# Two-block transformer kernel: the first block's attention, with the values as the stationary side and the weights transposed by a diagonal

## The chip, the cores and the metric

One NeuronCore of a Trainium2 chip runs the whole program. Its engines are TensorE (PE in the rows; PEld is its weight load), VectorE (DVE), ScalarE (ACT), GpSimd (POOL) and SyncE (SP), which issues most DMAs. The metric is the device time of one execution in microseconds, as the median of several runs.

## The reference

A model of two blocks of two layers each, on one sequence of 256 tokens with width 1024, all in float32. The change touches the dilated attention in the layers of the first block (8 heads of 64). For one query position, the three dilated patterns together amount to one softmax in which a key counts once for each pattern that reaches it; the kernel puts the logarithm of that count into an additive mask. What is computed there:

```python
s = jnp.einsum('bnqhd,bnkhd->bnhqk', qb, kb) * (Dh ** -0.5)
s = jnp.where(mask[None, :, None], s, -jnp.inf)
m = jnp.max(s, axis=-1, keepdims=True)
p = jnp.exp(s - m)
l = jnp.sum(p, axis=-1)
o = jnp.einsum('bnhqk,bnkhd->bnqhd', p, vb) / jnp.transpose(l, (0, 1, 3, 2))[..., None]
...
wts = jax.nn.softmax(jnp.stack(lses), axis=0)
return jnp.einsum('gbsh,gbshd->bshd', wts, jnp.stack(outs))
...
mixed = ga * (ya @ w_proj_att) + gb * (yb @ w_proj_mlstm)
x = x + mixed @ w_out
```

`ya` is the attention's output, `yb` that of a second branch (an mLSTM) that runs beside it.

## The kernel before

The weights of all layers come through three slots as chunks of 128 x 2048 float32. SyncE loads a chunk into `raw`, ScalarE copies it to the reduced format fp32r as `w_hi` (L158), VectorE subtracts to get `w_lo` (L165), and PE multiplies with three products (L189 to L191) that keep float32 accuracy. A feature chunk (`f_chunk`, called through `feature(i, c)`) is 48 such products, and its result is the projection of the activations with features in the partitions. The order of work on each engine is written out by hand: between two feature chunks PE does one small step of the attention or of the mLSTM, so that the other engines have the length of a chunk to answer. `Splitter.upto(c)` on ScalarE (`high`) and VectorE (`low`) splits chunks up to number c. Semaphores carry the dependencies; a `Signal` counts them over the layers.

The attention in one layer l goes like this. The 256 queries are two tiles `qt`; tile 0 sees one tile of keys, tile 1 sees two.

- VectorE evicts the values from PSUM into `v_tok`, with a column of ones behind each head's 64 values (L812).
- PE writes the scores (L1114). VectorE adds the mask (L894) and takes the row maxima (L899, L901). ScalarE takes the exponentials in place in `logit` (`soft(qt)`, L634), a head at a time.
- PE transposes the weights in 24 tiles of 128 x 128, in three groups of eight (`weights_T(0)` to `(2)`, L1159): groups 0 and 1 are tile 1 of the queries, group 2 is tile 0. ScalarE copies each group to `pT` (L683).
- PE multiplies the transposed weights, as the stationary side, with values and ones (L1184): 24 products of 65 columns. The result has tokens in the partitions, and column 64 of each head is the row sum.
- VectorE takes the reciprocals of the sums (L970), multiplies into `ya` (L975), and PE transposes `ya` in eight tiles (L1191) to put the features into the partitions. ScalarE and VectorE split that into `yH` and `yL` (L697, L984), which the projection chunks 23 to 26 read.

The gate chunks between these steps are numbers 17 to 22: `feature(8, 17)`, `weights_T(0)`, `feature(9, 18)`, `weights_T(1)` and the transposes of `hn` (L1170), `feature(10, 19)`, `weights_T(2)`, `feature(11, 20)`, the value products, `feature(12, 21)`, the transposes of `ya`, `feature(13, 22)`. Meanwhile VectorE normalises the mLSTM's output: it waits for ScalarE's copies of the numerators (L667, L668), squares (L935), and goes through a chain of small instructions to `hn` (L953), for which `weights_T(1)` waits on PE. GpSimd only issues four kinds of DMA in the first block.

Of the kernel before, what the change touches and what calls it, by code (L numbers as in the profile page):

```python
# [48 lines left out]

DVE_A = 112  # L50


CARRIED = {n: n for n in ("sc_done", "pT_done", "pT_ready", "pv_done", "max_ready", "exp_ready", "mix_ready", "mixH_ready",
                          "mix_split", "f_evicted")}
CARRIED.update(xT_done="qkT_done", uv_done="yaT_done", hT_done="hnT_done", rbc_done="nm_done", up0_done="s_done",
               xH_ready="qkF_ready", x_ready="ya_split", nH_ready="yaH_ready", n_ready="yb_split")
# [346 lines left out]
def head_slot(h):  # L403


    return h // 2, h % 2
# [3 lines left out]
def first_block(nc, k, d, sems, block):  # L410

    with ExitStack() as ctx:
# [3 lines left out]
        def sig(name, per, start=0):  # L416
# [26 lines left out]
                R3[:, MH * SEQ:MH * (SEQ + P)].rearrange("p (h n) -> p h n", h=MH)]  # L443
        v_tok = sb("v_tok", [P, TT, AH, AD + 1])
        mv_tok = sb("mv_tok", [P, TT, MH, MD + 1])
# [3 lines left out]
        hn = sb("hn", [P, TT * MH * MD])  # L449
        ya = sb("ya", [P, TT * AH * AD])  # L450
        hn_v = hn[:, :].rearrange("p (t h d) -> p (t h) d", t=TT, h=MH)
# [3 lines left out]
        num_out = lambda tt, h: three(tt)[:, h, :] if h < 3 else fourth[:, tt, :]  # L455
        ya_v = ya[:, :].rearrange("p (t j e d) -> p t j e d", t=TT, j=4, e=2)
        g_rows = hn[0:MH, :].rearrange("p (a n) -> p a n", a=4)
# [11 lines left out]
        nL = k.mixL[:, :].rearrange("p (f n) -> p f n", f=8)  # L469
        yH, yL = k.aH, k.aL  # L470
        junk = R2[:, 0:TT * DM].rearrange("p (t n) -> p t n", t=TT)
        s2 = sb("s2", [P, TT])
# [29 lines left out]
            sig("hn_ready", 1), sig("hnT_done", 1), sig("yb_ready", 1), sig("ybH_ready", 1), sig("yb_split", 1))  # L502
        pT_done, pT_ready, pv_done, ya_ready = sig("pT_done", 3), sig("pT_ready", 3), sig("pv_done", 1), sig("ya_ready", 1)
        yaT_done, yaH_ready, ya_split = sig("yaT_done", 1), sig("yaH_ready", 1), sig("ya_split", 1)
# [16 lines left out]
        def _(pool):  # L521
# [3 lines left out]
                .then_inc(row_loaded.sem, 16)  # L525
            pool.dma_start(consts[:, KA_ADD:KA_END], d.consts_a[:, KA_ADD:KA_END]).then_inc(const_loaded.sem, 16)
            for l in range(1, DEPTH):
                pool.wait_ge(t_evicted.sem, t_evicted.at(l - 1, 4))
                pool.wait_ge(gate_ready.sem, gate_ready.at(l - 1, 1))
                pool.dma_start(rows[:, :], d.rows_a[l:l + 1, :].rearrange("a n -> (a n)").partition_broadcast(P))\  # L530
                    .then_inc(row_loaded.sem, 16)
                pool.wait_ge(k.a_ready.sem, k.a_ready.at(l - 1, 12))
                pool.dma_start(par[:, :], d.par_a[l * P:(l + 1) * P, :]).then_inc(par_loaded.sem, 16)
                if l == 1:
                    pool.dma_start(hot, d.hot_b).then_inc(hot_loaded.sem, 16)
                    pool.dma_start(rel_sb, d.rel_bias).then_inc(hot_loaded.sem, 16)
                    pool.wait_ge(line_ready.sem, 1)
                    pool.dma_start(d.bias_line, line).then_inc(k.bias_moved, 16)
# [3 lines left out]

            pool.dma_start(k.par_b, d.par_b[0:P, :]).then_inc(k.par_b_loaded, 16)
            pool.wait_ge(k.a_ready.sem, k.a_ready.at(DEPTH - 1, 12))
            pool.dma_start(consts[:, KB_ADD:KB_END], d.consts_b[:, KB_ADD:KB_END]).then_inc(k.consts_b_loaded, 16)
# [20 lines left out]
        def _(act):  # L566
# [6 lines left out]
            for l in range(DEPTH):  # L573
# [40 lines left out]
                def conv_tanh(j):  # L614
                    act.wait_ge(conv_ready.sem, conv_ready.at(l, j + 1))
                    act.activation((hn, ya)[j][:, :], mqk[:, 4 * j:4 * j + 4, :].rearrange("p f n -> p (f n)"),
                                   ACT.Tanh, scale=0.5).then_inc(convt_ready.sem, 1)
# [12 lines left out]
                def soft(qt):  # L630

                    act.wait_ge(max_ready.sem, max_ready.at(l, 2 - qt))
                    for h in range(AH):
                        ins = act.activation(logit[qt][:, h, :], logit[qt][:, h, :], ACT.Exp,  # L634
                                             bias=rmax[:, qt, h:h + 1], scale=AD ** -0.5)
                    ins.then_inc(exp_ready.sem, 1)
# [94 lines left out]
        def _(dve):  # L731
            ch = Chain(k.pre_chain, 0)
            dve.memset(ones[:, :], 1.0).then_inc(k.pre_chain, 1)
            ch.n = 1
            dve.memset(v_tok[:, :, :, AD:AD + 1], 1.0).then_inc(ch.sem, ch.one())
            dve.memset(mv_tok[:, :, :, MD:MD + 1], 1.0).then_inc(ch.sem, ch.one())
# [31 lines left out]
            for l in range(DEPTH):  # L768
# [26 lines left out]
                for n in range(4):  # L795
                    dve.wait_ge(k.chunk_done, st.results(l, 2 * n + 1))
                    for tt in range(TT):
# [8 lines left out]
                        elif n == 2:  # L806
                            dst, src = v_tok[:, tt, :, 0:AD], src.rearrange("p (h d) -> p h d", h=8)
                            b = bias_rows(n).rearrange("p (h d) -> p h d", h=8)
# [44 lines left out]
                def conv_silu(j):  # L853

                    dve.wait_ge(convt_ready.sem, convt_ready.at(l, j + 1))
                    v = mqk[:, 4 * j:4 * j + 4, :].rearrange("p f n -> p (f n)")
                    dve.scalar_tensor_tensor(v, (hn, ya)[j][:, :], 1.0, v, ALU.add, ALU.mult).then_inc(mqk_ready.sem, 1)

# [65 lines left out]
                low.upto(17)  # L924
                row_max(0)
                low.upto(18)

                dve.wait_ge(num_copied.sem, num_copied.at(l, 1))
# [42 lines left out]
                dve.wait_ge(ch.sem, ch.at(l))  # L971
                for qt in range(TT):
                    for par_ in range(2):
                        src = k.ps[:, 4 + 2 * qt + par_, 0:4 * (AD + 1)].rearrange("p (j d) -> p j d", j=4)
                        ins = dve.tensor_tensor(ya_v[:, qt, :, par_, :], src[:, :, 0:AD],  # L975
                                                last(rsum[:, qt, 4 * par_:4 * par_ + 4], AD), ALU.mult)
# [68 lines left out]
        def _(pe):  # L1045
# [3 lines left out]
            for l in range(DEPTH):  # L1049
# [100 lines left out]
                def weights_T(i):  # L1150

                    for n, b in enumerate(((4, 5), (6, 7), (4, 5))[i]):
                        for s in range(4):
# [3 lines left out]
                            else:  # L1157
                                src = logit[0][:, 4 * n + s, :]
                            ins = pe.transpose(k.ps[:, b, s * P:(s + 1) * P], src, k.ident)  # L1159
                    ins.then_inc(pT_done.sem, 1)  # L1160
# [17 lines left out]
                pe.wait_ge(pT_ready.sem, pT_ready.at(l, 3))  # L1178
                for qt in range(TT):
# [12 lines left out]
                ins.then_inc(yaT_done.sem, 1)  # L1192
                feature(13, 22)
# [1507 lines left out]
```

## Time and profile before

| | |
|---|---|
| median of 3 runs | 1947.67 us (1947.66 to 1947.9) |
| the profiled execution | 1947.58 us |
| its span, first to last instruction | 1945.9 us |
| PE busy | 1926.0 us (99%) |
| PE weight loads busy | 1721.2 us (88%) |
| VectorE busy | 1379.2 us (71%) |
| ScalarE busy | 926.0 us (48%) |
| GpSimd busy | 238.2 us (12%) |

The 1.7 us between the span and the execution's time lie outside the instructions. Busy time is the time in which at least one instruction of the engine is in flight. Matmuls are pipelined, so the duration of one is longer than the step from one to the next, and a busy PE need not be at its peak.

### The profile page before, as it was taken

What the parts mean: (1) busy time and instruction counts of PE and PEld (TensorE: products, weight loads), DVE (VectorE), ACT (ScalarE), POOL (GpSimd) and SP (SyncE); (2) the same over time, 40 slices, a digit from 0 to 9 for tenths busy, and PEclk for the clock granted to TensorE, in tenths of its full rate; (3) what the DMA queues carried; (4) which work ended last, traced back from release to release, by engine and by line L of the source; (5) the groups of instructions that cost most, each with busy time, mean ns of one, the idle gap of its engine ahead of it and who ended that gap; (6) DMA issues with size and microseconds to landing.
All of it is one profiled execution on the core that took longest, in us unless ns stands there. A gap on an engine that the chain in (4) does not pass through costs nothing.

```text
span 1945.9 us, 29897 instructions
## 1 busy us (share of the span) xinstructions
PE 1926.0 (99%) x11936; PEld 1721.2 (88%) x11936; DVE 1379.2 (71%) x1577; ACT 926.0 (48%) x1020; POOL 238.2 (12%) x196
## 2 busy tenths in 40 slices
PE   7999999999999999999999999999999999999998
PEld 6999888889998888888899998888888899998887
DVE  7686766677677666766769677667766769677666
ACT  5564433445644443644554445444544554445443
POOL 0000000000001000000049250000000049250000
PEclk9999999999999999999999999999999999999999
DMA  7544555554355555555454455555555454555553
GB/s 269 195 159 152 188 184 192 195 192 173 132 195 205 194 192 175 186 191 181 167 183 152 171 190 191 185 194 175 205 192 181 167 183 152 173 190 180 185 192 108
DMA packets 50483, 353.37 MB, mean 182 GB/s; under 512 B 5921, under 2 KB 6049, under 8 KB 8657
## 3 DMA queue, kind: packets, MB, share of 16 engines
q1 hardware_dynamic: 47952, 341.93, 49.6%
q0 software_dynamic: 2432, 10.04, 1.6%
q8 instruction: 73, 1.20, 0.2%
q14 instruction: 26, 0.20, 0.0%
HBM read 349.85 MB, written 2.10 MB: 181 GB/s over the span
## 4 chain that ended last, share of the span: by engine, by line
PE 89%; DVE 6%; ACT 2%; issue 1%; DMA 0%; DVEq 0%; SPq 0%; POOL 0%; POOLq 0%; ACTq 0%
PE ps L225 19%; PE ps L189 18%; PE ps L191 18%; PE ps L190 18%; PE ps L226 9%; DVE w_lo L165 3%; PE ps L229 3%; PE ps L228 1%; ACT w_hi L158 1%; DVE conv_y L2021 1%; PE ps L1184 1%; DVE score L2069 0%; ACT a L1565 0%; PE ps L2202 0%; DVE top L2064 0%
## 5 line engine op out<-in xcount | busy, mean ns | idle before, releaser
L165 DVE TENSOR_TENSOR w_lo<-raw,w_hi 128x2048 fp32r<-128x2048 f32 x318 | 736.5, 2319 | 283.4 <-ACT w_hi L158 282.3
L158 ACT ACTIVATE w_hi<-raw 128x2048 fp32r<-128x2048 f32 x318 | 608.0, 1916 | 402.3 <-PE ps L191 225.7
L225 PE MATMUL ps<-a,w_hi 128*128 128x512 f32 x1568 | 563.2, 398 | 2.3 <-DVE w_lo L165 1.3
L226 PE MATMUL ps<-a,w_lo 128*128 128x256 f32 x1568 | 439.9, 281 | 0.0
L225 PEld LDWEIGHTS ps<-a,w_hi 128*128 128x128 f32 x1568 | 295.0, 188 | 67.5 <-DVE w_lo L165 2.4
L189 PE MATMUL ps<-mixH,w_hi 128*128 128x256 f32 x1168 | 334.4, 286 | 0.6 <-DVE w_lo L165 0.4
L190 PE MATMUL ps<-mixL,w_hi 128*128 128x256 f32 x1168 | 330.4, 283 | 0.0
L191 PE MATMUL ps<-mixH,w_lo 128*128 128x256 f32 x1168 | 330.3, 283 | 0.0
L189 PE MATMUL ps<-w_hi,mixH 128*128 128x512 f32 x832 | 324.9, 390 | 1.0 <-DVE mixL L397 0.9
L191 PE MATMUL ps<-w_hi,mixL 128*128 128x512 f32 x832 | 323.8, 389 | 0.0
L190 PE MATMUL ps<-w_lo,mixH 128*128 128x512 f32 x832 | 323.7, 389 | 0.0
L226 PEld LDWEIGHTS ps<-a,w_lo 128*128 128x128 f32 x1568 | 296.2, 189 | 9.0
L189 PEld LDWEIGHTS ps<-mixH,w_hi 128*128 128x128 f32 x1168 | 223.9, 192 | 4.1 <-issue 2.1
L190 PEld LDWEIGHTS ps<-mixL,w_hi 128*128 128x128 f32 x1168 | 224.0, 192 | 0.0
L191 PEld LDWEIGHTS ps<-mixH,w_lo 128*128 128x128 f32 x1168 | 223.9, 192 | 0.0
L191 PEld LDWEIGHTS ps<-w_hi,mixL 128*128 128x128 f32 x832 | 156.2, 188 | 32.9
L190 PEld LDWEIGHTS ps<-w_lo,mixH 128*128 128x128 f32 x832 | 156.3, 188 | 32.7
L189 PEld LDWEIGHTS ps<-w_hi,mixH 128*128 128x128 f32 x832 | 156.2, 188 | 31.4 <-DVE w_lo L165 1.3
L1620 ACT ACTIVATE GU<-GU 128x512 f32<-128x512 f32 x36 | 22.8, 632 | 185.5 <-DVE GU L1907 185.5
L1446 POOL TENSOR_TENSOR pss<-pss,neg_half 128x1 f32<-128x1 f32 x12 | 6.7, 560 | 742.8 <-DVE pss L1833 742.8
L229 PE MATMUL ps<-a,w_hi 128*128 128x512 f32 x224 | 89.1, 398 | 0.0
L1905 DVE TENSOR_REDUCE GU<-ps 128x512 f32<-128x1024 f32 x40 | 48.9, 1224 | 49.9 <-PE ps L229 49.9
(378 smaller groups left out, 2274.8 us busy)
## 6 DMA issues: line engine op xcount, KB each, us to landing
raw<-in_w_b SPq DMA_DIRECT2D x198, 1024.0 KB, 5.0
raw<-in_w_a SPq DMA_DIRECT2D x125, 1024.0 KB, 4.8
rows<-in_post_gains POOLq DMA_DIRECT2D x6, 512.0 KB, 4.1
rows<-in_rows_a POOLq DMA_DIRECT2D x2, 1028.0 KB, 7.1
raw<-in_w_a SPq DMA_DIRECT2D x2, 512.0 KB, 5.9
x<-in_x SPq DMA_DIRECT2D x2, 512.0 KB, 5.9
bias_line<-a_gates POOLq DMA_DIRECT2D x1, 1024.0 KB, 4.2
out<-x SPq DMA_DIRECT2D x4, 256.0 KB, 2.0
```

Source lines behind the costliest of these rows:

```text
L158: act.activation(k.w_hi[:, s, :], k.raw[:, s, :], ACT.Copy).then_inc(k.hi_ready, 1)
L165: dve.tensor_tensor(k.w_lo[:, s, :], k.raw[:, s, :], k.w_hi[:, s, :].bitcast(F32), ALU.subtract).then_inc(k.lo_ready, 1)
L189: pe.matmul(out, a[0], b[0], start=first, stop=False)
L190: pe.matmul(out, a[0], b[1], start=False, stop=False)
L191: return pe.matmul(out, a[1], b[0], start=False, stop=end)
L225: pe.matmul(both, hi[:, kt, cols], k.a[:, :, kt, :], start=kt == 0, stop=False)
L226: pe.matmul(high, lo[:, kt, cols], k.a[:, 0, kt, :], start=False, stop=False)
L228: pe.matmul(high, lo[:, kt, cols], k.a[:, 0, kt, :], start=False, stop=False)
L229: end = pe.matmul(both, hi[:, kt, cols], k.a[:, :, kt, :], start=False, stop=True)
L1184: ins = pe.matmul(out, pT[:, 4 * e + j, s + qt, :], v_tok[:, s, h, :], start=s == 0, stop=s == qt)
L1620: act.activation(hid_r[:, j % 2, :], hid_r[:, j % 2, :], ACT.Silu).then_inc(silu_ready.sem, 1)
L1905: dve.tensor_reduce(r, halves(k, 4 if j == 1 else 0), AX.X, ALU.add).then_inc(asum_ready.sem, 1)
```

## The change

- `v_tok` gets 128 columns for each head instead of 65. It is cleared once; a head with an even number has its values in columns 0 to 63, one with an odd number in 64 to 127, and the other half stays zero. So the eviction on VectorE takes four instructions instead of two.
- The exponentials on ScalarE also give their row sums (`accum_out`) into `rsum`. VectorE takes the reciprocals in SBUF (`row_inverse`), once for each query tile.
- GpSimd multiplies the identity with the reciprocals into eight diagonals for each query tile (`row_diagonals`), in the space of `mqk`, which is free by then.
- `weights_T` multiplies by these diagonals instead of transposing, so that the transposed weights come out normalised.
- The values are now the stationary side. For each pair of heads four products accumulate into one 128 x 256 result with the features in the partitions: for key tile 0 two products of 256 columns, one for each head, and for key tile 1 two of 128 columns, for the second query tile alone.
- The multiplications into `ya`, `ya` itself and its transposes are gone. One place where `ya` served as scratch (`conv_tanh(1)`) uses R2.

```diff
-        v_tok = sb("v_tok", [P, TT, AH, AD + 1])
+        v_tok = sb("v_tok", [P, TT, AH, 2 * AD])
+        v_own = v_tok[:, :, :, :].rearrange("p t (j e) d -> p t j e d", e=2)
...
+        rdiag = [mqk[:, 4 * (1 - qt):4 * (2 - qt), :].rearrange("p f n -> p (f n)").rearrange("p (h n) -> p h n", h=AH)
+                 for qt in range(TT)]
...
+            def row_diagonals(l):
+
+                for i, qt in enumerate((1, 0)):
+                    pool.wait_ge(rinv_ready.sem, rinv_ready.at(l, i + 1))
+                    pool.tensor_tensor(rdiag[qt], mid(k.ident, AH), last(rsum[:, qt, :], P), ALU.mult).then_inc(rdiag_ready.sem, 1)
+
...
+                row_diagonals(l - 1)
...
                         ins = act.activation(logit[qt][:, h, :], logit[qt][:, h, :], ACT.Exp,
-                                             bias=rmax[:, qt, h:h + 1], scale=AD ** -0.5)
+                                             bias=rmax[:, qt, h:h + 1], scale=AD ** -0.5,
+                                             accum_out=rsum[:, qt, h:h + 1])
...
-            dve.memset(v_tok[:, :, :, AD:AD + 1], 1.0).then_inc(ch.sem, ch.one())
+            dve.memset(v_tok[:, :, :, :], 0.0).then_inc(ch.sem, ch.one())
...
+                            for e in range(2):
+                                ins = dve.tensor_tensor(v_own[:, tt, :, e, e * AD:(e + 1) * AD], src[:, :, e, :], b[:, :, e, :], ALU.add)
...
+                def row_inverse(qt):
+
+                    dve.wait_ge(exp_ready.sem, exp_ready.at(l, 2 - qt))
+                    dve.reciprocal(rsum[:, qt, :], rsum[:, qt, :]).then_inc(rinv_ready.sem, 1)
+
                 low.upto(18)
+                row_inverse(1)
...
                 dve.tensor_tensor(hn_v, hn_v, last(y_, MD), ALU.mult).then_inc(hn_ready.sem, 1)
+                row_inverse(0)
...
-                dve.wait_ge(pv_done.sem, pv_done.at(l, 1))
-                for qt in range(TT):
-                    for par_ in range(2):
-                        src = k.ps[:, 4 + 2 * qt + par_, 0:4 * (AD + 1)].rearrange("p (j d) -> p j d", j=4)
-                        dve.reciprocal(rsum[:, qt, 4 * par_:4 * par_ + 4], src[:, :, AD]).then_inc(ch.sem, ch.one())
...
-                ins.then_inc(ya_ready.sem, 1)
                 low.upto(22)
+                dve.wait_ge(pT_done.sem, pT_done.at(l, 3))
...
                 def weights_T(i):
 
+                    pe.wait_ge(rdiag_ready.sem, rdiag_ready.at(l, 2 if i == 2 else 1))
...
-                            ins = pe.transpose(k.ps[:, b, s * P:(s + 1) * P], src, k.ident)
+                            ins = pe.matmul(k.ps[:, b, s * P:(s + 1) * P], src, rdiag[1 if i < 2 else 0][:, h, :], start=True, stop=True)
...
-                for qt in range(TT):
-                    for h in range(AH):
-                        j, e = head_slot(h)
-                        out = k.ps[:, 4 + 2 * qt + e, j * (AD + 1):(j + 1) * (AD + 1)]
-                        for s in range(qt + 1):
-                            ins = pe.matmul(out, pT[:, 4 * e + j, s + qt, :], v_tok[:, s, h, :], start=s == 0, stop=s == qt)
-                ins.then_inc(pv_done.sem, 1)
+                for j in range(AH // 2):
+                    out = k.ps[:, 4 + j // 2, (j % 2) * SEQ:(j % 2 + 1) * SEQ]
+                    pe.matmul(out, v_tok[:, 0, 2 * j, :], pT[:, j, 0:2, :], start=True, stop=False)
+                    for e in range(2):
+                        pe.matmul(out[:, P:SEQ], v_tok[:, 1, 2 * j + e, :], pT[:, 4 * e + j, 2, :], start=False, stop=False)
+                    ins = pe.matmul(out, v_tok[:, 0, 2 * j + 1, :], pT[:, 4 + j, 0:2, :], start=False, stop=True)
+                ins.then_inc(yaT_done.sem, 1)
                 feature(12, 21)
-
-                pe.wait_ge(ya_ready.sem, ya_ready.at(l, 1))
-                for f in range(4):
-                    for tt in range(TT):
-                        ins = pe.transpose(k.ps[:, 4 + f // 2, (f % 2) * SEQ + tt * P:(f % 2) * SEQ + (tt + 1) * P], ya[:, tt * 512 + f * P:tt * 512 + (f + 1) * P], k.ident)
-                ins.then_inc(yaT_done.sem, 1)
                 feature(13, 22)
```

The order of the built instructions shows two places in the words of the program. The first is PE in layer 0, at the value products between chunks 20 and 21 (R is the space that holds `pT`; in brackets stand the semaphores an instruction waits for). Before:

```order
L191 MATMUL ps<-mixH,w_lo 128x256
L1184 MATMUL ps<-v_tok,R 128x65 [waits a_pT_ready]
L1184 MATMUL ps<-v_tok,R 128x65 x23
L189 MATMUL ps<-mixH,w_hi 128x256 [waits a_f_evicted,lo_ready]
...
L191 MATMUL ps<-mixH,w_lo 128x256
L1191 MATMUL ps<-consts,ya 128x128 [waits a_ya_ready]
L1191 MATMUL ps<-consts,ya 128x128 x7
L189 MATMUL ps<-mixH,w_hi 128x256 [waits a_f_evicted,lo_ready]
```

After (the three product rows L1195, L1197 and L1198 stand four times in a row, once for each pair of heads):

```order
L191 MATMUL ps<-mixH,w_lo 128x256
L1195 MATMUL ps<-R,v_tok 128x256 [waits a_pT_ready]
L1197 MATMUL ps<-R,v_tok 128x128 x2
L1198 MATMUL ps<-R,v_tok 128x256
L1195 MATMUL ps<-R,v_tok 128x256
...
L189 MATMUL ps<-mixH,w_hi 128x256 [waits a_f_evicted,lo_ready]
```

The 24 narrow products became 16 wider ones, and chunks 21 and 22 now follow each other with nothing between them. The second place is VectorE in layer 0, behind the split of chunk 18. Before:

```order
L165 TENSOR_TENSOR w_lo<-raw,w_hi 128x2048 [waits hi_ready]
L932 COPY small<-ps 128x3 [waits a_num_copied]
L932 COPY small<-ps 128x3
L933 COPY small<-ps 128x2
L935 TENSOR_TENSOR R<-hn 128x1024
```

After:

```order
L165 TENSOR_TENSOR w_lo<-raw,w_hi 128x2048 [waits hi_ready]
L945 RECIPROCAL rsum<-rsum 128x8 [waits a_exp_ready]
L954 COPY small<-ps 128x3 [waits a_num_copied]
L954 COPY small<-ps 128x3
L955 COPY small<-ps 128x2
L957 TENSOR_TENSOR R<-hn 128x1024
```

A reciprocal with a wait of its own stands ahead of the wait for the numerators; GpSimd's first multiplication waits for it.

## Rows read from the trace of the kernel before

**Rows 1.** The page: span, and busy us, share of the span, instructions.
```profile
span 1945.9 us, 29897 instructions
...
PE 1926.0 (99%) x11936; PEld 1721.2 (88%) x11936; DVE 1379.2 (71%) x1577; ACT 926.0 (48%) x1020; POOL 238.2 (12%) x196
```

**Rows 2.** PE's waits, whole span: us in total, times, longest.
```profile
PE ps L360 <- DVEq L766: 9.2, 1, 9.2
```

**Rows 3.** Windows: busy us of each engine, PE clock, DMA share, GB/s.
```profile
core 0: us, PE busy (x) PEld busy (x) DVE busy (x) ACT busy (x) POOL busy (x), PEclk, DMA share, GB/s
126.90:165.60 38.70, 38.70 (x332) 38.70 (x332) 22.51 (x31) 18.17 (x24) 0.00 (x0) 1.00 0.39 137
```

**Rows 4.** Groups by line and shape on PE: busy us, mean ns, idle before.
```profile
L1184 PE MATMUL ps<-v_tok,R 128*128 128x65 f32 x96 | 10.9, 274 | 0.0
...
L1159 PE MATMUL ps<-consts,R 128*128 128x128 f32 x48 | 6.2, 272 | 0.0
...
L2398 PE MATMUL ps<-consts,y 128*128 128x128 f32 x16 | 2.1, 274 | 0.0
```

**Rows 5.** The chain of waits in order of time: start us, us, what.
```profile
110.31 1.73 PE ps L1133 x8
112.04 0.89 PE ps L1136 x8
...
127.11 0.87 PE ps L1159 x8
128.10 0.12 PE ps L190
133.74 0.87 PE ps L1159 x8
...
141.24 0.87 PE ps L1159 x8
147.86 5.30 PE ps L1184 x48
...
158.97 0.87 PE ps L1191 x8
...
1105.01 0.89 PE ps L2398 x8
```

**Rows 6.** Timeline of ACT: start, us, line, what, idle before.
```profile
114.38 3.31 ACT L634 ACTIVATE R<-R,rmax 128x256 f32<-128x256 f32 x8 [0.23 <-DVE rmax L901]
118.73 0.84 ACT L645 ACTIVATE a_gates<-ps,a_par 128x256 f32<-128x256 f32 x2 [1.03 <-PE ps L191]
...
1095.24 0.19 ACT L1761 ACTIVATION_READ_ACCUMULATOR conv_y<-y 128x1 f32 x1
1095.34 0.40 ACT L1761 ACTIVATE conv_y<-y 128x256 f32<-128x256 f32 x1
```

**Rows 7.** Timeline of DVE in layer 0, behind the split of chunk 18.
```profile
119.53 2.29 DVE L165 TENSOR_TENSOR w_lo<-raw,w_hi 128x2048 fp32r<-128x2048 f32 x1
122.59 0.23 DVE L932 COPY small<-ps 128x3 f32<-128x3 f32 x2 [0.77 <-ACT hn L668]
...
122.80 1.21 DVE L935 TENSOR_TENSOR R<-hn 128x1024 f32<-128x1024 f32 x1
...
128.68 1.23 DVE L953 TENSOR_TENSOR hn<-hn,small 128x1024 f32<-128x1024 f32 x1
```

**Rows 8.** Timeline of POOL and DVE in the second block.
```profile
1137.46 1.30 POOL L1525 TENSOR_TENSOR GU<-GU 128x512 f32<-128x512 f32 x1
...
1140.54 3.23 POOL L1527 TENSOR_TENSOR GU<-GU 128x512 f32<-128x512 f32 x1
...
1140.01 2.60 DVE L165 TENSOR_TENSOR w_lo<-raw,w_hi 128x2048 fp32r<-128x2048 f32 x1 [0.70 <-ACT w_hi L158]
```

**Rows 9.** Timeline of DVE at the start of the program.
```profile
0.94 0.27 DVE L733 MEMSET ones<- 128x256 f32 x1 [0.94 <-PEq L2691]
...
3.44 0.17 DVE L738 CAST pos_f<-pos_i 128x2 f32<-128x2 int32 x1 [2.18 <-DMA consts<-in_consts_a]
```

More of the change, by code:

```diff
@@ L48 @@
 AHEAD_HIGH, AHEAD_LOW = 2, 1
-DVE_A = 112
-CARRIED = {n: n for n in ("sc_done", "pT_done", "pT_ready", "pv_done", "max_ready", "exp_ready", "mix_ready", "mixH_ready",
+DVE_A = 108
+CARRIED = {n: n for n in ("sc_done", "pT_done", "pT_ready", "max_ready", "exp_ready", "mix_ready", "mixH_ready",
                           "mix_split", "f_evicted")}
-CARRIED.update(xT_done="qkT_done", uv_done="yaT_done", hT_done="hnT_done", rbc_done="nm_done", up0_done="s_done",
+CARRIED.update(pv_done="rinv_ready", xT_done="qkT_done", uv_done="yaT_done", hT_done="hnT_done", rbc_done="nm_done", up0_done="s_done",
                xH_ready="qkF_ready", x_ready="ya_split", nH_ready="yaH_ready", n_ready="yb_split")
@@ L449, in first_block @@
         hn = sb("hn", [P, TT * MH * MD])
-        ya = sb("ya", [P, TT * AH * AD])
+        tanh1 = R2[:, 0:TT * AH * AD]
         hn_v = hn[:, :].rearrange("p (t h d) -> p (t h) d", t=TT, h=MH)
@@ L455, in first_block @@
         num_out = lambda tt, h: three(tt)[:, h, :] if h < 3 else fourth[:, tt, :]
-        ya_v = ya[:, :].rearrange("p (t j e d) -> p t j e d", t=TT, j=4, e=2)
         g_rows = hn[0:MH, :].rearrange("p (a n) -> p a n", a=4)
@@ L502, in first_block @@
             sig("hn_ready", 1), sig("hnT_done", 1), sig("yb_ready", 1), sig("ybH_ready", 1), sig("yb_split", 1))
-        pT_done, pT_ready, pv_done, ya_ready = sig("pT_done", 3), sig("pT_ready", 3), sig("pv_done", 1), sig("ya_ready", 1)
+        pT_done, pT_ready, rinv_ready, rdiag_ready = sig("pT_done", 3), sig("pT_ready", 3), sig("rinv_ready", 2), sig("rdiag_ready", 2)
         yaT_done, yaH_ready, ya_split = sig("yaT_done", 1), sig("yaH_ready", 1), sig("ya_split", 1)
@@ L543, in _ @@
             pool.dma_start(k.par_b, d.par_b[0:P, :]).then_inc(k.par_b_loaded, 16)
+            row_diagonals(DEPTH - 1)
             pool.wait_ge(k.a_ready.sem, k.a_ready.at(DEPTH - 1, 12))
@@ L615, in conv_tanh @@
                     act.wait_ge(conv_ready.sem, conv_ready.at(l, j + 1))
-                    act.activation((hn, ya)[j][:, :], mqk[:, 4 * j:4 * j + 4, :].rearrange("p f n -> p (f n)"),
+                    act.activation((hn, tanh1)[j][:, :], mqk[:, 4 * j:4 * j + 4, :].rearrange("p f n -> p (f n)"),
                                    ACT.Tanh, scale=0.5).then_inc(convt_ready.sem, 1)
@@ L806, in _ @@
                         elif n == 2:
-                            dst, src = v_tok[:, tt, :, 0:AD], src.rearrange("p (h d) -> p h d", h=8)
-                            b = bias_rows(n).rearrange("p (h d) -> p h d", h=8)
+                            src = src.rearrange("p (j e d) -> p j e d", j=4, e=2)
+                            b = bias_rows(n).rearrange("p (j e d) -> p j e d", j=4, e=2)
+                            for e in range(2):
+                                ins = dve.tensor_tensor(v_own[:, tt, :, e, e * AD:(e + 1) * AD], src[:, :, e, :], b[:, :, e, :], ALU.add)
+                            continue
                         else:
@@ L856, in conv_silu @@
                     v = mqk[:, 4 * j:4 * j + 4, :].rearrange("p f n -> p (f n)")
-                    dve.scalar_tensor_tensor(v, (hn, ya)[j][:, :], 1.0, v, ALU.add, ALU.mult).then_inc(mqk_ready.sem, 1)
+                    dve.scalar_tensor_tensor(v, (hn, tanh1)[j][:, :], 1.0, v, ALU.add, ALU.mult).then_inc(mqk_ready.sem, 1)
                 conv(0)
@@ L964, in _ @@
                 low.upto(21)
-                dve.wait_ge(pv_done.sem, pv_done.at(l, 1))
-                for qt in range(TT):
-                    for par_ in range(2):
-                        src = k.ps[:, 4 + 2 * qt + par_, 0:4 * (AD + 1)].rearrange("p (j d) -> p j d", j=4)
-                        dve.reciprocal(rsum[:, qt, 4 * par_:4 * par_ + 4], src[:, :, AD]).then_inc(ch.sem, ch.one())
-                dve.wait_ge(ch.sem, ch.at(l))
-                for qt in range(TT):
[L973 to L976, printed above, removed]
-                ins.then_inc(ya_ready.sem, 1)
                 low.upto(22)
+                dve.wait_ge(pT_done.sem, pT_done.at(l, 3))
                 dve.wait_ge(ybH_ready.sem, ybH_ready.at(l, 1))
@@ L1157, in weights_T @@
                             else:
-                                src = logit[0][:, 4 * n + s, :]
-                            ins = pe.transpose(k.ps[:, b, s * P:(s + 1) * P], src, k.ident)
+                                h = 4 * n + s
+                                src = logit[0][:, h, :]
+                            ins = pe.matmul(k.ps[:, b, s * P:(s + 1) * P], src, rdiag[1 if i < 2 else 0][:, h, :], start=True, stop=True)
                     ins.then_inc(pT_done.sem, 1)
@@ L1178, in _ @@
                 pe.wait_ge(pT_ready.sem, pT_ready.at(l, 3))
-                for qt in range(TT):
-                    for h in range(AH):
-                        j, e = head_slot(h)
-                        out = k.ps[:, 4 + 2 * qt + e, j * (AD + 1):(j + 1) * (AD + 1)]
-                        for s in range(qt + 1):
-                            ins = pe.matmul(out, pT[:, 4 * e + j, s + qt, :], v_tok[:, s, h, :], start=s == 0, stop=s == qt)
-                ins.then_inc(pv_done.sem, 1)
-                feature(12, 21)
-                pe.wait_ge(ya_ready.sem, ya_ready.at(l, 1))
-                for f in range(4):
-                    for tt in range(TT):
-                        ins = pe.transpose(k.ps[:, 4 + f // 2, (f % 2) * SEQ + tt * P:(f % 2) * SEQ + (tt + 1) * P], ya[:, tt * 512 + f * P:tt * 512 + (f + 1) * P], k.ident)
-                ins.then_inc(yaT_done.sem, 1)
+                for j in range(AH // 2):
[5 more added lines that the diff above has]
+                ins.then_inc(yaT_done.sem, 1)
+                feature(12, 21)
                 feature(13, 22)
```

## The prediction, made before the changed kernel ran

> **What bounds the kernel now.** I read the page first: TensorE is busy for 1926.0 us of a span of 1945.9 us, while VectorE has 71% [rows 1]. Then the waits of PE: the longest is 9.2 us at the very start, for the first loads, and nothing in the first block's attention is on that list [rows 2]. Then the busy time by windows over the stretch that the diff touches in layer 0, from the first weight transposes at 126.9 us to the end of the last gate product at 165.6 us: PE is busy for all 38.70 us, at a granted clock of 1.00, the level of 2.4 GHz [rows 3]; layer 1 runs the same instructions. So here PE is never waiting, not even for VectorE between the value products (L1184) and the transposes of `ya` (L1191), because a whole gate chunk stands between them. Whatever PE issues more is paid in full, and whatever others do less is worth nothing.
>
> A duration of a matmul in the trace overlaps its neighbours (274 ns of one at L1184 [rows 4]), so it is no price. The chain of waits gives the price, since it lists by how much one piece moves the next: 48 passes of L1184 in 5.30 us, 0.110 us each [rows 5]. The counts in the groups by shape show what a pass is: L1184 has 24 products in each of two layers and 96 records, so a plain f32 product is two passes; L1159 has 24 transposes in each layer and 48 records, so a transpose is one; L2398, which in the second block multiplies by a diagonal just as the change does, has 8 products and 16 records [rows 4].
>
> **The change on PE, for one layer.**
> (1) 24 transposes become 24 products with a diagonal. A transpose of 128 columns costs 0.87 / 8 = 0.109 us. The diagonal product costs two passes of 0.89 / 8 = 0.111 us, by L2398 (the same operation) and by L1136 (another f32 product of 128 columns) [rows 5]. The three groups of eight go from 3 x 0.87 = 2.61 to 3 x 16 x 0.111 = 5.34 us: +2.73.
> (2) The value products. Before, 24 products of 65 columns took 5.30 us. Sixty-five columns cost 0.110 and 128 cost 0.111 us, so narrow products had no advantage, and that is what the new form can win back. After, there are 8 products of 256 columns and 8 of 128. A 256-column pass costs 1.73 / 8 = 0.216 us (L1133 [rows 5]). So 16 x 0.216 + 16 x 0.111 = 3.46 + 1.78 = 5.24 us: -0.06. Half of the stationary columns are zeros, so twice the columns are worked through to save passes, and the two nearly cancel.
> (3) The eight transposes of `ya` go: -0.87 [rows 5].
> Sum: 2.73 - 0.06 - 0.87 = +1.80 us a layer, +3.6 us for two. All of it is on PE's path.
>
> A rule of the Trainium skill would price this otherwise. TensorE: Matmul & The Clock Gate, section "Back-to-back issue gap", gives columns / 2.4 + 2.5 ns, so 56 ns for 128 columns, 109 for 256, 30 for 65. An estimate by that page is 24 x 56 = +1.34, -0.45 for the `ya` transposes, and 2.64 against 1.42 us for the value products, so +2.1 us a layer and about 1951.8 us. The rows for f32 here are twice its figures at 128 and 256 columns and nearly four times at 65, so the rows decide.
>
> **The change on the other engines.** All of this must stay hidden under PE.
> ScalarE: 16 exponentials a layer now also read out a sum. Where the second block does that at 256 columns, the next activation starts 0.10 us after the read-out does (1095.24 to 1095.34), so eight add 0.8 us. The first group starts at 114.38 and lasts 3.31; behind it the engine idles 1.03 us for PE [rows 6], which covers it.
> VectorE: the first reciprocal goes behind the weight split that starts at 119.53 and lasts 2.29, into the 0.77 us in which VectorE waits for the copies of the numerators. Its input, the exponentials, is there at 117.7 + 0.8 = 118.5. It costs some 0.2 us and is done at about 122.0 [rows 7]. Queued behind it is the chain to `hn`, whose last instruction starts at 128.68 and ends at 129.9, and which PE wants at 133.74 (later after the change): 3.8 us of cover. The second reciprocal stands behind `hn`. The four reciprocals and four multiplications on PSUM behind L1184 vanish. VectorE's next splits come earlier and nobody waits for them. The value eviction in four pieces and the wait for the transposes ahead of the low half of `yb` lie in idle time.
> GpSimd: a multiplication with 1024 elements a partition, twice a layer, a step that had no predecessor. Its nearest row is 512 elements in 1.30 us undisturbed and 3.23 us at worst, when a 2.60 us weight split was running on VectorE [rows 8]. So 2.6 to 6.5 us. The first diagonal starts at 122.0 and is ready between 124.6 and 128.5; PE asks for it with the first transposes, at 127.1 [rows 5]. I take 2.6, because VectorE has just gone idle when GpSimd starts. Then the slack is 2.5 us and the wait costs nothing. At 6.5 us the wait would be 1.4 us a layer. The second diagonal starts near 130 to 132 and is wanted at 141.24 plus 1.8: hidden even at 6.5 us. The memory loads in GpSimd's queue behind these waits are wanted a hundred us later.
> The Trainium skill, SBUF — State Buffer, section "SBUF: two separate sides", says that GpSimd and a VectorE instruction with two SBUF inputs lock each other out for a whole instruction, whoever starts first. By that rule it is VectorE's squaring at 122.80 that is held until 124.6, so `hn` comes about 2 us later, still inside its 3.8 us: no change to the sum. The 3.23 us row agrees with it.
> Start: clearing `v_tok` takes 2048 elements instead of 16. At 256 elements in 0.27 us that is about 2.1 us from 1.2 us on, while VectorE waits until 3.44 for its first load [rows 9]. Hidden, barely; behind it there is slack too.
>
> **Sum.** The profiled execution took 1947.58 us; 1947.58 + 3.6 = 1951.2 us. The median of the runs is 1947.67, so that is +0.18%. About 0.2% (3.9 us, a time of 1951.6) is what a measurement of this kernel can tell from no change, so the forecast lies just inside.
>
> **The rivals.**
> A, the sum, 1950.4 to 1951.5: chance 0.59. For it: PE without a gap, and each price from a row of the same form.
> B, the diagonal comes late. Place: PE in front of the first transposes, L1173 in the changed kernel. Price at the bound 1.4 us a layer, so 1947.58 + 3.6 + 2.8 = 1954.0 us, slower. It decides from the point at which the GpSimd multiplication takes over 5.1 us, or begins that much later. For it: GpSimd with a broadcast operand of zero stride is shown nowhere here, and its spans swing by 2.5 times. Against it: VectorE is idle when it starts. Chance 0.12.
> C, the same mechanism as A but a little dearer: the passes of the diagonal or the 256-column ones cost 2% more, or each change between formats costs 0.05 us, so 1951.6 to 1952.4 us, slower by a hair. Chance 0.20.
> D, wide products cheaper. The 256-column passes of the reduced format (L189 to L191) move on by 0.12 us [rows 5]; if the new ones, with their contiguous operands, came near that, the value products would take 16 x 0.12 + 1.78 = 3.7 us and the sum would be 1.80 - 1.54 = +0.26 us a layer, 1948.1 us. Against it: L1133 has the same form and costs 0.216. Chance 0.06.
> E, the change takes away a stall that the trace doesn't show, or the diagonal costs one pass (1951.2 - 5.3 = 1945.9, still within 0.2%). For a real gain, below 1943.8, both D and this would be needed. Chance 0.03 together.
>
> **How the numbers follow.** Faster takes 0.03. Within 0.2%: A and D, 0.65. Slower: B and C, 0.32. The likeliest is A, 1951.2. The range runs from 1949.6, which leaves D and E out (0.09), to 1954.4, which takes in the bound of B.
>
> **What would show it.** In the changed kernel the chain should show L1173 at 1.78 us for each group of 16 passes, the value lines (L1195 to L1198) at 5.24 us, no transposes of `ya`, and the stretch from the first transposes to the end of the last gate product 1.8 us longer than 38.70. PE's waits should not name GpSimd. GpSimd's two rows should read near 2.6 us, with the first one done before 125. ScalarE's exponentials should be followed by read-outs and still end before 118.8. I am wrong if PE waits ahead of L1173, if 256 columns with values as the stationary side cost other than 0.216, or if the time moves by something outside this stretch.

## The result, and the profile after

The changed kernel takes 1950.76 us (median of 20 runs, 1950.5 to 1951.51), the one before 1947.62 us (20 runs, 1947.22 to 1947.93). The ratio is 1.0016, with a 95% interval of 1.0011 to 1.0022: 3.1 us more. The profiled execution took 1950.5 us, its span is 1948.8 us.

First the page of the kernel after, with busy us, share and instructions. PE has the same number of instructions and is busy for 3.3 us more; it is still the only engine near its limit.

```profile
span 1948.8 us, 29933 instructions
...
PE 1929.3 (99%) x11936; PEld 1725.1 (89%) x11936; DVE 1383.9 (71%) x1569; ACT 928.5 (48%) x1052; POOL 249.2 (13%) x200
```

The chain of waits of the kernel after, in layer 0 (start us, us, what), answers to [rows 5].

```profile
127.02 1.78 PE ps L1173 x16
134.56 1.78 PE ps L1173 x16
136.35 0.87 PE ps L1184 x8
142.97 1.78 PE ps L1173 x16
150.51 0.43 PE ps L1195 x2
150.94 0.44 PE ps L1197 x4
151.39 0.43 PE ps L1198 x2
...
155.32 0.43 PE ps L1198 x2
```

Each group of eight transposes (0.87 us) has become 16 passes in 1.78 us. The value products, of which four such sets stand in a row, run from 150.51 to 155.75, so 5.24 us where there were 5.30. Behind them the two gate chunks follow each other; the 0.87 us for `ya` are gone. The waits of PE (us in total, times, longest) name nothing in this stretch, as before:

```profile
PE ps L360 <- DVEq L778: 9.1, 1, 9.1
PE ps L225 <- DVE w_lo L165: 1.3, 5, 0.6
```

Where the time went can be read from three points of the two chains and timelines. PE reaches the first transposes 0.09 us earlier than before (127.02 against 127.11; its first wait, for the loads, is 0.1 us shorter). ScalarE's eviction behind the last gate product of the layer starts at 167.30, where it started at 165.63 (the kernel before, then the one after):

```profile
165.63 0.84 ACT L645 ACTIVATE a_gates<-ps,a_par 128x256 f32<-128x256 f32 x2 [2.86 <-PE ps L191]
```
```profile
167.30 0.84 ACT L657 ACTIVATE a_gates<-ps,a_par 128x256 f32<-128x256 f32 x2 [2.14 <-PE ps L191]
```

So the stretch is 1.67 + 0.09 = 1.76 us longer, and the same again in layer 1. That is 3.5 us; the difference of the two profiled executions is 2.9. The rest of the way is the same but for one place, in the second block's first layer, which gives 0.44 us back (below, one multiplication on GpSimd).

The timelines of the other engines in layer 0 (start us, us, line, what, idle before) show that the cover held.

```profile
118.16 0.19 ACT L645 ACTIVATION_READ_ACCUMULATOR R<-R,rmax 128x1 f32 x1
118.64 0.84 ACT L657 ACTIVATE a_gates<-ps,a_par 128x256 f32<-128x256 f32 x2 [0.29 <-PE ps L191]
```
```profile
121.64 0.19 DVE L945 RECIPROCAL rsum<-rsum 128x8 f32<-128x8 f32 x1
122.49 0.23 DVE L954 COPY small<-ps 128x3 f32<-128x3 f32 x2 [0.66 <-ACT hn L680]
...
122.70 2.19 DVE L957 TENSOR_TENSOR R<-hn 128x1024 f32<-128x1024 f32 x1
...
129.56 1.23 DVE L975 TENSOR_TENSOR hn<-hn,small 128x1024 f32<-128x1024 f32 x1
130.70 0.19 DVE L945 RECIPROCAL rsum<-rsum 128x8 f32<-128x8 f32 x1
130.81 2.24 DVE L165 TENSOR_TENSOR w_lo<-raw,w_hi 128x2048 fp32r<-128x2048 f32 x1
132.97 2.38 DVE L979 TENSOR_SCALAR mo<-mo 128x1024 f32<-128x1024 f32 x1
```
```profile
121.92 1.89 POOL L534 TENSOR_TENSOR mqk<-consts,rsum 128x1024 f32<-128x1024 f32 x1 [31.61 <-DVE rsum L945]
130.97 3.84 POOL L534 TENSOR_TENSOR mqk<-consts,rsum 128x1024 f32<-128x1024 f32 x1 [7.16 <-DVE rsum L945]
```

ScalarE's idle time ahead of the gate eviction shrinks from 1.03 to 0.29 us. The first diagonal is ready at 123.8, 3.2 us before PE asks. VectorE's squaring takes 2.19 instead of 1.21 us and ends at 124.9, and the scaling of `mo` 2.38 us where it took 0.68 before: both overlap a GpSimd multiplication. Likewise the second multiplication lasts twice as long as the first: a weight split of VectorE (L165, 130.81 to 133.05) had started 0.16 us before it. `hn` is ready at 130.8, 0.9 us later than before, with 3.8 us to go until PE wants it at 134.56.

### The profile page after: what moved, and what is told of

It is laid out like the page before. It is cut to its first block, busy times and chain, and to the rows that moved or that the text cites. A ratio compares the mean times of both kernels' runs of the same rounds, so it can differ in the third digit from the quotient of the medians.

```text
span 1948.8 us, 29933 instructions
## 1 busy us (share of the span) xinstructions
PE 1929.3 (99%) x11936; PEld 1725.1 (89%) x11936; DVE 1383.9 (71%) x1569; ACT 928.5 (48%) x1052; POOL 249.2 (13%) x200
## 4 chain that ended last, share of the span: by engine, by line
PE 89%; DVE 7%; ACT 2%; issue 1%; DMA 0%; DVEq 0%; SPq 0%; POOL 0%; POOLq 0%; ACTq 0%
PE ps L225 19%; PE ps L189 18%; PE ps L191 17%; PE ps L190 17%; PE ps L226 9%; PE ps L229 3%; DVE w_lo L165 3%; PE ps L228 1%; DVE conv_y L2029 1%; ACT w_hi L158 1%; PE ps L1173 1%; DVE score L2077 1%; ACT a L1573 0%; DVE top L2072 0%; PE ps L2210 0%
## 5 line engine op out<-in xcount | busy, mean ns | idle before, releaser
L165 DVE TENSOR_TENSOR w_lo<-raw,w_hi 128x2048 fp32r<-128x2048 f32 x318 | 736.9, 2321 | 289.8 <-ACT w_hi L158 288.8
```

The costliest lines, as they stand in the source:

```text
L165: dve.tensor_tensor(k.w_lo[:, s, :], k.raw[:, s, :], k.w_hi[:, s, :].bitcast(F32), ALU.subtract).then_inc(k.lo_ready, 1)
```

## The experiments

**PE's passes, or the new waits?** (e1_transposes) The diagonals are made and waited for, but PE transposes with the identity, so the division by the row sums is left out.

```diff
-                            ins = pe.matmul(k.ps[:, b, s * P:(s + 1) * P], src, rdiag[1 if i < 2 else 0][:, h, :], start=True, stop=True)
+                            ins = pe.transpose(k.ps[:, b, s * P:(s + 1) * P], src, k.ident)
```

> The changed kernel with its 24 diagonal products a layer put back to plain transposes. The diagonals are still made and PE still waits for them, but they aren't used, so the division by the row sums is left out. Theory (PE pays for each pass at the step of the chain, everything else is hidden): 3 groups of eight go from 1.78 to 0.87 us, so 2 x 2.73 = 5.5 us less than the changed kernel, 1945.3 us, which is 2.3 us below the kernel before. Rival (the extra time comes from the wait for GpSimd, the read-outs on ScalarE or VectorE's delays): all these stay, so the time stays at 1950.8 us.

Measured: 1945.44 us (11 runs), ratio to the kernel before 0.9989, interval 0.998 to 0.9998. The chain shows the groups at 0.87 us again and the value products unchanged. The whole loss of the change, and 2.2 us more, sits in the second pass of the diagonal products. The waits and the other engines cost nothing.

**That edit alone, on the kernel before.** (e2_products_only)

```diff
-                            ins = pe.transpose(k.ps[:, b, s * P:(s + 1) * P], src, k.ident)
+                            ins = pe.matmul(k.ps[:, b, s * P:(s + 1) * P], src, k.ident, start=True, stop=True)
```

> The kernel before with one edit: the 24 weight transposes a layer are plain f32 products with the identity. Nothing else of the change is in it: no GpSimd, no row sums on ScalarE, no wide value products. Theory: two passes of 0.111 us instead of one of 0.109 us, so +2.73 us a layer, 1947.6 + 5.5 = 1953.1 us. Rival (the passes are cheap and the loss of the change lies in the value products with half of their columns zero): less than 1950 us.

Measured: 1952.9 us (8 runs), ratio 1.0028 (1.0017 to 1.0038), 5.3 us more. Its chain, beside the old value products:

```profile
127.22 1.78 PE ps L1159 x16
...
150.69 5.30 PE ps L1184 x48
156.00 0.17 PE ps L189
```

So the term is the same from both sides, +5.3 here and -5.3 in the first experiment. The last row is a small cost that I had left out: the first gate product behind these narrow f32 products takes 0.17 us of the chain instead of 0.12.

**Do narrow products cost their columns?** (e3_columns_128) The kernel before with 128 moving columns a head.

```diff
-        v_tok = sb("v_tok", [P, TT, AH, AD + 1])
+        v_tok = sb("v_tok", [P, TT, AH, 2 * AD])
...
-                        out = k.ps[:, 4 + 2 * qt + e, j * (AD + 1):(j + 1) * (AD + 1)]
+                        out = k.ps[:, 4 + 2 * qt + e, j * 2 * AD:(j + 1) * 2 * AD]
```

> The kernel before with 128 columns moving per head in the value products instead of 65 (64 values and 64 ones); for space, ya lies in mqk and the scratch of the second tanh in R2, as in the changed kernel. Theory: a pass costs 0.110 us at 65 columns and 0.111 us at 128, so 48 x 0.001 us a layer, no change: 1947.6 to 1947.8 us. Rival (a pass costs its columns / 2.4 + 2.5 ns, as the Trainium skill's page TensorE: Matmul & The Clock Gate has it in its section Back-to-back issue gap): 48 passes a layer with 63 more columns at 26 ns, so +2.5 us in all, 1950.1 us; if a column costs the two cycles that 128 and 256 columns show, +5 us.

Measured: 1947.73 us (11 runs), ratio 1.0 (0.9991 to 1.0009). The interval reaches up to 1.8 us, so the rival's 2.5 us lie outside it, and the chain is finer. It has the 48 passes at 5.36 us, against 5.30 at 65 columns:

```profile
147.78 5.36 PE ps L1185 x48
158.89 0.87 PE ps L1192 x8
```

Twice the columns cost 0.001 us a pass. The kernel before has a row with 64 moving columns too, in the second block, at 0.108 us a pass:

```profile
1001.70 1.73 PE ps L2385 x16
```

So from 64 to 128 columns the step is nearly the same. Why isn't tested; each of these passes comes with a weight load of 128 columns.

By the formula of the Trainium skill (TensorE: Matmul & The Clock Gate, "Back-to-back issue gap"), 63 more columns are 26 ns a pass, and these f32 products don't follow it. But that section gives the formula for an isolated matmul, and says that in a stream of matmuls with weight loads it is too low for few columns: 81 ns are measured there at 128. The prediction and the expectation above used it without this restriction. The 81 ns are not the 111 ns of these rows either.

**How much cover do the diagonals have, and what does a late one cost?** (e8, e9 and e4, with the first diagonals of a layer made twice, three times and four times.) The edit for four:

```diff
+                    for n in range(3 if i == 0 else 0):
+                        pool.tensor_tensor(rdiag[qt], mid(k.ident, AH), last(rsum[:, qt, :], P), ALU.mult).then_inc(again.sem, 1)
+                        pool.wait_ge(again.sem, again.at(l, n + 1))
                     pool.tensor_tensor(rdiag[qt], mid(k.ident, AH), last(rsum[:, qt, :], P), ALU.mult).then_inc(rdiag_ready.sem, 1)
```

Four times:

> The changed kernel with the first diagonals of each layer made four times over by GpSimd, one after the other, before they are announced. Theory: in the changed kernel the first one runs from 121.9 to 123.8 us and PE asks at 127.0, so 3.2 us are free; four take at least 4 x 1.9 = 7.6 us, end at 129.5 or later, and PE waits at least 2.5 us a layer, so 1955.8 us or more, and PE's list of waits names GpSimd. Where VectorE's splits hold GpSimd up (3.8 us for one multiplication in the changed kernel), it is up to 4 x 3.8 us, and 1970 us. Rival (the diagonals have far more cover than that, or PE doesn't really stand on them): 1950.8 us.

Twice:

> The changed kernel with the first diagonals of each layer made twice. In the kernel that made them four times, the multiplications ended about 1.9, 4.7, 6.7 and 8.7 us after the start. Theory: twice ends 4.7 us after 121.9, at 126.7, just ahead of PE's 127.0, so no wait and 1950.8 us. Rival (the cover is less than the 3.2 us read from the profile): PE waits in front of L1177 and the time rises by more than 0.5 us.

Three times:

> The changed kernel with the first diagonals of each layer made three times: ready at about 121.9 + 6.8 = 128.7 us, so PE waits 1.7 us a layer. Theory one, as my prediction priced a late diagonal (the wait alone counts): 1950.8 + 3.4 = 1954.2 us. Theory two (as in the kernel with four, where the granted clock behind a wait of 3.75 us was 0.50 and the 16 passes took 3.40 instead of 1.78 us): a wait of 1.7 us is followed by a stretch at half the clock too, and the time is 1956 us or more. The clock by windows tells them apart.

| made | time, us (runs) | ratio to before, interval | GpSimd ready | PE starts | PE's wait a layer |
|---|---|---|---|---|---|
| once | 1950.76 (20) | 1.0016 (1.0011 to 1.0022) | 123.8 | 127.0 | 0 |
| twice | 1950.7 (10) | 1.0017 (1.0008 to 1.0026) | 126.5 | 126.8 | 0 |
| three times | 1954.67 (5) | 1.0037 (1.0024 to 1.005) | 128.6 | 128.7 | 1.8 |
| four times | 1962.87 (5) | 1.0078 (1.0064 to 1.0092) | 131.0 | 131.2 | 3.7 |

Doubling the suspected cost changes nothing: the cover is real. With three, little more than the wait is paid: PE waits 3.5 us in all, and the 16 passes behind it take 2.02 us on the chain instead of 1.78, so 4.0 us, where the time rises by 3.9. With four, PE waits 7.5 us in all and the time rises by 12.1. Of the other 4.6 us, 3.4 stand right behind the waits: from the first group of diagonal products to the next it takes 1.6 us longer than in the changed kernel in layer 0, and 1.8 in layer 1. With three that was 0.24 us a layer, at full clock, so some 2.9 of the 3.4 us are the clock. The last 1.2 us lie outside the attention (0.4 us ahead of it, where PE's first wait is 0.3 us longer in this profile, and the rest behind layer 1), and their cause stays open. The windows of the kernel with four (stretch, us, PE busy, granted clock, DMA) and then its timeline behind the wait:

```profile
115.00:127.00 12.00, 12.00 (x104) 1.00 0.63 230
...
131.00:132.00 1.00, 0.84 (x4) 0.50 0.00 0
132.00:133.00 1.00, 1.00 (x7) 0.50 0.00 0
133.00:134.00 1.00, 1.00 (x6) 0.50 0.00 0
134.00:136.00 2.00, 2.00 (x19) 0.99 0.00 0
...
519.00:523.00 4.00, 4.00 (x24) 0.59 0.00 0
```
```profile
131.16 3.40 PE L1177 MATMUL ps<-mqk,R 128*128 128x128 f32 x16 [3.75 <-POOL mqk L538]
```

Behind the wait of 3.75 us the granted clock is 0.50, the level of 1.2 GHz; on the chain the 16 passes take 3.40 us instead of 1.78, and layer 1 shows the same with 0.59 over 4 us (2.84 us for its 16 passes). In the kernel with three, behind 1.76 us of waiting, the windows show 1.00, in layer 1 too:

```profile
129.00:130.00 1.00, 1.00 (x11) 1.00 0.00 0
130.00:131.00 1.00, 1.00 (x11) 1.00 0.00 0
```

The two expectations for three stood against each other; theory one holds.

**The division in another place.** (e5_scale_in_place) Nothing is left out. GpSimd scales the weights in three pieces and PE transposes them.

```diff
-                for i, qt in enumerate((1, 0)):
-                    pool.wait_ge(rinv_ready.sem, rinv_ready.at(l, i + 1))
-                    pool.tensor_tensor(rdiag[qt], mid(k.ident, AH), last(rsum[:, qt, :], P), ALU.mult).then_inc(rdiag_ready.sem, 1)
+                for i, (qt, heads) in enumerate(((1, slice(0, 4)), (1, slice(4, 8)), (0, slice(0, 8)))):
+                    pool.wait_ge(rinv_ready.sem, rinv_ready.at(l, 1 if qt else 2))
+                    part = logit[qt][:, heads, :]
+                    pool.tensor_tensor(part, part, last(rsum[:, qt, heads], part.shape[-1]), ALU.mult).then_inc(rdiag_ready.sem, 1)
...
-                    pe.wait_ge(rdiag_ready.sem, rdiag_ready.at(l, 2 if i == 2 else 1))
+                    pe.wait_ge(rdiag_ready.sem, rdiag_ready.at(l, i + 1))
```

> The changed kernel with the division done in another place: GpSimd multiplies the weights themselves by the reciprocal row sums, in place in logit, in three pieces of 1024 elements a partition (heads 0 to 3 and 4 to 7 of the second query tile, then the first tile), and PE transposes them with the identity as before the change. Nothing is left out. Theory (PE pays for passes alone; GpSimd is hidden as long as each piece is there in time): the first piece takes 1.9 to 2.6 us from 121.9 and is wanted at 127.0, the second is wanted at 133.7, the third at 141.2; so 5.5 us less than the changed kernel, 1945.3 us, ratio 0.9988 to the kernel before. Rival (two pieces in a row on GpSimd hold up VectorE's chain to hn, or come late themselves): PE waits in front of the transposes and the gain shrinks or turns, 1946 to 1951 us.

Measured: 1945.31 us (11 runs), ratio 0.9989 (0.998 to 0.9998). PE waits for none of the pieces.

```profile
121.78 4.72 POOL L535 TENSOR_TENSOR R<-R,rsum 128x1024 f32<-128x1024 f32 x2 [31.61 <-DVE rsum L946]
132.41 3.84 POOL L535 TENSOR_TENSOR R<-R,rsum 128x1024 f32<-128x1024 f32 x1 [5.90 <-DVE rsum L946]
```

**The zeros out of the value products.** (e6_halves)

```diff
-                    pe.matmul(out, v_tok[:, 0, 2 * j, :], pT[:, j, 0:2, :], start=True, stop=False)
-                    for e in range(2):
-                        pe.matmul(out[:, P:SEQ], v_tok[:, 1, 2 * j + e, :], pT[:, 4 * e + j, 2, :], start=False, stop=False)
-                    ins = pe.matmul(out, v_tok[:, 0, 2 * j + 1, :], pT[:, 4 + j, 0:2, :], start=False, stop=True)
+                    half = [slice(e * AD, (e + 1) * AD) for e in range(2)]
+                    for e in range(2):
+                        pe.matmul(out[half[e]], v_tok[:, 0, 2 * j + e, half[e]], pT[:, 4 * e + j, 0:2, :], start=True, stop=False)
+                    for e in range(2):
+                        ins = pe.matmul(out[half[e], P:SEQ], v_tok[:, 1, 2 * j + e, half[e]], pT[:, 4 * e + j, 2, :], start=False, stop=True)
```

> The changed kernel with the zeros out of the value products: each head's product uses 64 stationary columns and writes 64 partitions, the even head of a pair the lower and the odd head the upper ones, and the two stand next to each other. The number of products and of moving columns stays. Rival one (a pass costs what its moving columns cost, whatever its width): the value products stay at 5.24 us a layer and the time at 1950.8 us. Rival two (two products on different halves of the array run side by side, as the page TensorEngine Tiling (Array Packing) of the Trainium skill says of column tiling in its section Overview, up to twofold): 2.6 us a layer less, 1945.6 us. The scores of this kernel (L1114), which use different halves of the rows, support the second: 16 passes of 256 and 16 of 128 columns take 2.82 us, where 16 x 0.216 + 16 x 0.111 would be 5.24.

Measured: 1946.36 us (11 runs), ratio 0.9994 (0.9985 to 1.0003), 4.4 us less than the changed kernel. Rival two, less two small costs that the chain shows at the ends:

```profile
150.55 0.58 PE ps L1197 x4
151.13 0.22 PE ps L1199 x4
151.35 0.43 PE ps L1197 x4
...
153.09 0.22 PE ps L1199 x4
153.30 0.32 PE ps L189
```

Four passes of 256 columns take 0.43 us, where two on the whole array took that. In the trace they start in pairs, one of each head, 0.01 us apart, and the next pair 0.22 us later, so this isn't a cheaper narrow pass: the heads of a pair run side by side, as TensorEngine Tiling (Array Packing) of the Trainium skill has it in "Overview". The first four take 0.15 us more, and the first gate product behind them 0.32 instead of 0.12. So 5.24 becomes 2.75 us, and 0.2 behind it.

**Both together.** (e7_both) The edits of e5_scale_in_place and e6_halves.

> Both edits together: the weights scaled in place by GpSimd and transposed by PE, and value products on halves of the array. Nothing of the computation is left out. If the effects add, the time is the changed kernel's less what each of the two takes off: 1950.8 - 5.5 - 5.2 = 1940.1 us where halves run side by side, 1945.3 where they don't. If PE then catches up with another engine, it waits for it and the sum of the two isn't reached.

Measured: 1940.7 us (5 runs), ratio to the kernel before 0.9966 (0.9952 to 0.9979). The two add: 1950.8 - 5.4 - 4.4 = 1941.0. This version beats both kernels, by 6.9 and 10.1 us.

**One multiplication on GpSimd.** (e10_one_on_gpsimd) The question was the 0.44 us in the second block. The kernel before, with this ahead of GpSimd's loop:

```diff
+            pool.wait_ge(x_free.sem, x_free.at(0, 1))
+            pool.tensor_tensor(pool_try[:, :], pool_try[:, :], pool_try[:, :], ALU.mult)
             for l in range(1, DEPTH):
```

> The kernel before with one GpSimd multiplication of 8 elements a partition on a scratch tile at its start, behind its first three DMAs; nothing reads its result. It asks why the second block's stretch from the value products to the diagonal products in its first layer takes 27.12 us in the kernel before and in the two without GpSimd arithmetic in the first block, and 26.7 in all those that have it. Theory: that GpSimd is used in the first block at all decides it, so here the stretch takes 26.7 and the time is 1947.2 us. Rival: it is the changed length of the attention ahead of it or the order on VectorE, and the stretch keeps its 27.12, 1947.6 us.

Measured: 1947.15 us (11 runs), ratio 0.9999 (0.999 to 1.0008), which can't tell 0.4 us; the chain can. The value products of the second block start at 1077.58 and the diagonal ones at 1104.27, so 26.69 us, where the changed kernel has 26.68 and the kernel before 27.12 (1077.89 to 1105.01). The chain of this run, then the first row of the kernel before:

```profile
1077.58 2.62 PE ps L2453 x24
...
1104.27 0.89 PE ps L2403 x8
```
```profile
1077.89 2.62 PE ps L2448 x24
```

What happens there is a race for access between GpSimd and VectorE. In the kernel before, this pair overlaps; the addition on GpSimd is held, and later a split of 3.28 us keeps PE waiting for 0.3 us:

```profile
1081.75 3.12 POOL L1503 TENSOR_TENSOR sum<-sum 128x538 f32<-128x538 f32 x1
```
```profile
1081.64 2.28 DVE L165 TENSOR_TENSOR w_lo<-raw,w_hi 128x2048 fp32r<-128x2048 f32 x1
```

In the changed kernel GpSimd is first, takes 1.08 us, and PE waits for nothing there:

```profile
1084.81 1.08 POOL L1511 TENSOR_TENSOR sum<-sum 128x538 f32<-128x538 f32 x1
```
```profile
1085.00 3.04 DVE L165 TENSOR_TENSOR w_lo<-raw,w_hi 128x2048 fp32r<-128x2048 f32 x1
```

What decides the race stands two instructions earlier. GpSimd's first addition there waits for VectorE's `conv_y`. In the kernel before it starts 0.44 us after VectorE's last row has ended, in the changed kernel 0.15 us after:

```profile
1079.22 1.28 POOL L1498 TENSOR_TENSOR conv_y<-conv_y,sum 128x512 f32<-128x512 f32 x1 [10.67 <-DVE conv_y L2021]
```
```profile
1082.29 1.28 POOL L1506 TENSOR_TENSOR conv_y<-conv_y,sum 128x512 f32<-128x512 f32 x1 [10.38 <-DVE conv_y L2029]
```

All three kernels without GpSimd arithmetic in the first block have the late start and 27.12 us; all nine with it, this one included, have the early start and 26.7 us. So the 0.44 us go with what GpSimd is given in the first block. Whether it is the arithmetic, or only more instructions in its program, isn't separated (this run adds a wait on GpSimd and a clearing on VectorE besides the multiplication), and how it acts 900 us later stays open.

## Why the prediction was right

- What bounds the kernel. PE without a gap in this stretch, and everything that it issues more is paid in full: shown from both sides, by the first two experiments.
- The diagonal products. Sum: +2.73 us a layer, by two passes of 0.111 us for one of 0.109. The chain has 1.78 for each group, and the edit alone costs 5.3 us in two layers, where 5.5 was expected.
- The value products. Sum: 5.24 us; measured 5.24. That 65 columns cost what 128 do was read from two rows and is shown by its own experiment. It is why the new form wins nothing here: the zeros cost as much as the wider products save.
- The transposes of `ya`. Sum: -0.87; they are gone and nothing has taken their place.
- The sum was +1.80 us a layer, the stretch gives +1.76. The mis-sized term is what stands between products of different formats: the gate product behind L1184 took 0.05 us more than a step, and this is gone. The forecast of 1951.2 adds 3.6 us for the two layers. The two stretches give 3.5, and the second block gives 0.4 back: 3.1 us, which is what the medians show. That part wasn't foreseen: I had named a time that moves outside this stretch as a sign of being wrong, and it does so, by an eighth of the forecast rise. "Within 0.2%" had most of the chance, and 0.16% is that; that the kernel is slower all the same is plain from 20 runs of each.
- GpSimd. I bounded the multiplication from 2.6 to 6.5 us and took 2.6. The first took 1.89, below the lower end. The lower end was twice a row of 512 elements, and this overstates it: rows with two full operands take 1.28 us at 512 elements (L1506) and 1.08 at 538 (L1511), so neither the time per element nor the price of a repeated operand can be had from one row. The second took 3.84. The cover of 2.5 us was right in kind and is 3.2 us in fact.
- Rival B, the late diagonal, didn't happen. I priced it at the wait alone. That nearly holds for 1.8 us of waiting, but at 3.7 us the passes behind the waits add 3.4 us to the 7.5, most of it by the clock, so with the first diagonals ready nine microseconds after their start my price would have been 4.6 us too low.
- VectorE's delay of `hn` while GpSimd has the access to SBUF: expected about 2 us, measured 0.9. Agreement on the mechanism; the difference is that the multiplication was shorter.
- Rivals D and E (256-column passes at the price of the reduced format, or a diagonal in one pass): refuted by the rows, 0.216 and 0.111 us a pass.

## What to carry to other kernels

Price TensorE by the step from one pass to the next in rows of the same format and shape, never by durations or columns: here a plain f32 product is two passes where a transpose is one, and a pass of 64 or 65 columns costs what one of 128 does. When a scale can go on an engine that has time, don't fold it into a transpose: the fold cost 5.3 us, the separate scaling on GpSimd nothing. And where half of a stationary operand would be zeros, put two products side by side on the halves of the array instead.

## What the runs showed of the hardware

- A GpSimd multiplication of 1024 elements a partition takes 1.89 us when it starts alone, both for the identity by a repeated reciprocal and as the first of the three in-place pieces (1.9 and 2.9 us in a pair of 4.72), and 3.84 us when a weight split of VectorE is already running.
- VectorE's scaling of one operand (`mo`, 1024 elements, 0.68 us alone) was stretched to 2.38 us beside a GpSimd multiplication; so not only instructions with two SBUF operands are held.
- TensorE's granted clock stayed at 1.00 behind a wait of 1.76 us and was 0.50 behind one of 3.75 us, where 16 passes took 3.40 instead of 1.78 us (2.84 in layer 1).
- A ScalarE exponential with a row sum costs 0.09 us more than one without (at 256 columns, eight of them take 0.74 us more of the engine's time).
- Column halves of the array: 0.15 us to enter and 0.2 us behind, for a stretch that shrinks from 5.24 to 2.75 us.
